# First mixer's recurrence in another order: row exponents one step ahead, norm factors right behind their moments, two half output tiles between the chunks

## The reference

```python
def even_mixer(h, w_in, w_out, sinks, conv_w, conv_b, i_bias, f_bias, ml_norm):
    p = h @ w_in
    ...
    y_att = sliding_window_sink_attention(q, k, v, sinks)
    ...
    hm = mlstm_chunkwise(q_m, k_m, v_m, log_i, log_f)
    hm = head_layernorm(hm, ML_NORM_EPS).reshape(bsz, T, ML_V_W) * ml_norm.astype(F32)
    y_ml = (hm * jax.nn.sigmoid(o_m.astype(F32))).astype(h.dtype)
    return jnp.concatenate([y_att, y_ml], axis=-1) @ w_out

# mlstm_chunkwise, 4 chunks of 128 tokens, 4 heads:
    C_loc = jnp.einsum('bnlh,bnlhk,bnlhv->bnhkv', wgt, kc, vc)
    C_new = fa[..., None, None] * C + fb[..., None, None] * Cl      # scan over the chunks
    w_intra = jnp.exp(dlog - m_t[:, :, :, None, :])
    w_inter = jnp.exp(inter_log - m_t)
    qk = jnp.einsum('bnthd,bnshd->bntsh', qc, kc) * w_intra
    num = jnp.einsum('bntsh,bnshv->bnthv', qk, vc) + w_inter[..., None] * jnp.einsum('bnthk,bnhkv->bnthv', qc, C_prev)
    h = num / jnp.maximum(jnp.abs(den), jnp.exp(-m_t))[..., None]
```

## Time and profile before

| | us |
|---|---|
| median of 3 runs | 1400.3 |
| lowest, highest | 1399.03, 1401.03 |
| the profiled execution | 1397.91 |
| its span in the profile | 1395.7 |
| PE busy in the span | 1324.3 (95%) |
| POOL, DVE, ACT busy | 662.4, 572.2, 537.6 |

### The profile page before, as it was taken

One profiled execution on the slowest core, in us unless ns is written; L12 is line 12 of the kernel. 1 busy time (PEld: TensorE's weight loads), 2 busy tenths in 40 slices (PEclk: granted clock), 3 DMA queues, 4 the chain that ended last, 5 costly groups with the idle time before them and its releaser, 6 DMA issues.

```text
span 1395.7 us, 17823 instructions
## 1 busy us (share of the span) xinstructions
PE 1324.3 (95%) x6461; PEld 1060.2 (76%) x6461; DVE 572.2 (41%) x917; ACT 537.6 (39%) x880; POOL 662.4 (47%) x813
## 2 busy tenths in 40 slices
PE   5999878999999999999798999888999999999997
PEld 4777656788888888887476778888878888888886
DVE  4537655421221211345679956365542121121233
ACT  5335654332322323335653436433443132231332
POOL 4653224554555545664343532321455555555552
PEclk9999978999999999999899999999999999999999
DMA  9322101333333333332212211000233333333331
GB/s 277 91 76 61 61 1 46 92 91 98 98 91 91 90 99 97 90 90 79 73 46 61 76 56 37 1 2 1 61 95 102 91 91 91 93 102 90 91 91 61
DMA packets 198034, 109.12 MB, mean 78 GB/s; under 512 B 4570, under 2 KB 195280, under 8 KB 197840
## 3 DMA queue, kind: packets, MB, share of 16 engines
q1 hardware_dynamic: 197552, 108.16, 26.4%
q0 software_dynamic: 416, 0.07, 0.0%
HBM read 106.11 MB, written 2.10 MB: 78 GB/s over the span
## 4 chain that ended last, share of the span: by engine, by line
PE 84%; DVE 9%; ACT 4%; issue 2%; DMA 0%; POOL 0%; DVEq 0%; SPq 0%; ACTq 0%
PE ps L878 23%; PE ps L879 23%; PE ps L880 23%; PE ps L865 2%; PE ps L919 1%; PE ps L920 1%; PE ps L921 1%; DVE arena L2273 1%; DVE late L2486 1%; PE ps L1283 1%; PE ps L1297 1%; PE ps L1036 1%; PE ps L1308 1%; PE ps L1165 1%; DVE arena L2559 0%
## 5 line engine op out<-in xcount | busy, mean ns | idle before, releaser
L782 POOL TENSOR_TENSOR w_lo<-raw_w,w_hi 128x256 fp32r<-128x256 f32 x760 | 616.4, 842 | 610.9 <-ACT w_hi L1405 610.9
L1405 ACT ACTIVATE w_hi<-raw_w 128x1024 fp32r<-128x1024 f32 x190 | 201.1, 1059 | 548.8 <-PE ps L880 439.7
L878 PE MATMUL ps<-hn_hi,w_hi 128*128 128x512 f32 x880 | 358.2, 407 | 3.0 <-POOL w_lo L782 2.1
L879 PE MATMUL ps<-hn_lo,w_hi 128*128 128x512 f32 x880 | 350.3, 398 | 0.0
L880 PE MATMUL ps<-hn_hi,w_lo 128*128 128x512 f32 x880 | 350.1, 398 | 0.0
L878 PE MATMUL ps<-hid_hi,w_hi 128*128 128x512 f32 x576 | 228.4, 397 | 0.0
L880 PE MATMUL ps<-hid_hi,w_lo 128*128 128x512 f32 x576 | 228.4, 396 | 0.0
L879 PE MATMUL ps<-hid_lo,w_hi 128*128 128x512 f32 x576 | 228.4, 396 | 0.0
L878 PEld LDWEIGHTS ps<-hn_hi,w_hi 128*128 128x128 f32 x880 | 167.1, 190 | 52.1 <-issue 10.6
L879 PEld LDWEIGHTS ps<-hn_lo,w_hi 128*128 128x128 f32 x880 | 166.9, 190 | 41.7 <-issue 2.9
L880 PEld LDWEIGHTS ps<-hn_hi,w_lo 128*128 128x128 f32 x880 | 166.7, 189 | 40.7
(11 more groups left out here) (376 smaller groups left out, 1343.5 us busy)
## 6 DMA issues: line engine op xcount, KB each, us to landing
raw_w<-in_w_up SPq DMA_DIRECT2D x64, 512.0 KB, 3.9
raw_w<-in_w_down SPq DMA_DIRECT2D x64, 512.0 KB, 3.6
raw_w<-in_o_w_in SPq DMA_DIRECT2D x27, 512.0 KB, 3.6
raw_w<-in_e_w_in SPq DMA_DIRECT2D x19, 512.0 KB, 3.6
raw_w<-in_e_w_out SPq DMA_DIRECT2D x8, 512.0 KB, 3.6
raw_w<-in_o_w_out SPq DMA_DIRECT2D x8, 512.0 KB, 3.4
rwkv_raw<-in_x SPq DMA_DIRECT2D x4, 512.0 KB, 8.1
out<-arena SPq DMA_DIRECT2D x8, 256.0 KB, 2.9
```

The source lines that it names most:

```text
L782: nc.gpsimd.tensor_tensor(w_lo[:, n % CUT, ks], raw_w[:, n % RING, ks], w_hi[:, n % CUT, ks].bitcast(F32), ALU.subtract).then_inc(w_cut, 1)
L878: mm(o, a_hi, b_hi, start=(k == 0), stop=False)
L879: mm(o, a_hi, b_lo, start=False, stop=False)
L1405: A(w_hi[:, n % CUT], raw_w[:, n % RING], ACT.Copy).then_inc(w_high, 1)
```

## The change

No instruction is added or removed on any engine; four things move.

1. ScalarE's list in `even_front`: `q_exp 1` goes from unit 7 to the end of unit 6, `w_exp 0` from unit 8 to unit 7. `w_exp 1` stays in unit 8. `w_exp` 2 and 3 leave units 9 and 10 and go behind the four copies of `hid_hi`, which become an item of their own (`att_high`).
2. TensorE's list and the plan of banks come from a new generator, `even_chunks`: `half_tile` 0 stands between `c_loc 2` and `num 2`, `half_tile` 1 between `qk_st 3` and `num 3`, 2 and 3 at the end.
3. VectorE: weights 1 and moments 0 come before the `low_first` four. `ml_gains(0)` stands between the second and third of these. Every later gains n follows its own moments n at once.
4. GpSimd: instead of four times L799 and then three times L806, each gain multiply is followed by the multiply with its normed chunk.

```diff
@@ -202,14 +202,28 @@
         if u == 9:
             for a in range(2):
                 yield "k_tok", a
-        if u == 7:
+        if u == 6:
             yield "q_exp", 1
-        if u == 8:
-            yield "w_exp", 0
-            yield "w_exp", 1
+        if u in (7, 8):
+            yield "w_exp", u - 7
         if u in (9, 10):
             yield "q_exp", u - 7
-            yield "w_exp", u - 7
+    yield "att_high", 0
+    yield "w_exp", 2
+    yield "w_exp", 3
+
+
+def even_chunks():
+
+    for n in range(NT):
+        yield "qk_st", n
+        if n < NT - 1:
+            yield "c_loc", n
+        if n >= 2:
+            yield "half", n - 2
+        yield "num", n
+    yield "half", 2
+    yield "half", 3
 
 
 def odd_front():
@@ -331,17 +345,18 @@
...
-            for n in range(NT):
-                for par in range(2):
-                    put("qk_st", n, par, bank=5 + par)
-                if n < NT - 1:
-                    put("c_loc", n, bank=7)
-                for par in range(2):
-                    put("num", n, par, bank=1 + 2 * (n % 2) + par)
-                if n == 1:
-                    put_out(0, 0)
-            for j in range(1, 4):
-                put_out(0, j)
+            for item in even_chunks():
+                kind, n = item
+                if kind == "half":
+                    put_out(0, n)
+                else:
+                    for par in range(2):
+                        if kind == "qk_st":
+                            put(kind, n, par, bank=5 + par)
+                        elif kind == "num":
+                            put(kind, n, par, bank=1 + 2 * (n % 2) + par)
+                    if kind == "c_loc":
+                        put(kind, n, bank=7)
             put_turned(0, "y_ml")
@@ -798,14 +813,14 @@
                         for t in range(NT):
                             nc.gpsimd.tensor_tensor(o_gate[:, t, :], o_gate[:, t, :], row("ml_norm", 512), ALU.mult
                                                     ).then_inc(S["o_gained"], 1)
-                        for t in range(NT - 1):
-
-                            pool.wait_ge(S["o_gained"], t + 1)
-                            drained(pool, "num", t, 0)
-                            drained(pool, "num", t, 1)
-                            nc.gpsimd.tensor_tensor(o_gate[:, t, :], o_gate[:, t, :],
-                                                    w_ml[:, t].rearrange("p h t -> p (h t)"), ALU.mult
-                                                    ).then_inc(S["y_ml_gated"], 1)
+                            if t < NT - 1:
+
+                                pool.wait_ge(S["o_gained"], t + 1)
+                                drained(pool, "num", t, 0)
+                                drained(pool, "num", t, 1)
+                                nc.gpsimd.tensor_tensor(o_gate[:, t, :], o_gate[:, t, :],
+                                                        w_ml[:, t].rearrange("p h t -> p (h t)"), ALU.mult
+                                                        ).then_inc(S["y_ml_gated"], 1)
                     if n == base["out", 1] + CUT - 1:
 
                         def zero_inverses(n):
@@ -1069,17 +1084,20 @@
                 for j in range(4):
                     drained(pe, "v", j)
                 pe.wait_ge(S["v_ones"], 1)
-                for n in range(NT):
+                for kind, n in even_chunks():
                     tok = slice(n * P, (n + 1) * P)
...
-                    if n < NT - 1:
+                    if kind == "half":
+                        half_tile(0, n, 0)
+                    elif kind == "qk_st":
+                        o = [free(pe, "qk_st", n, par) for par in range(2)]
+                        for a in range(2):
+                            for par in range(2):
...
+                    elif kind == "c_loc":
                         pe.wait_ge(S["k_scaled"], 1)
...
-                    pe.wait_ge(S["qkw_ready"], n + 1)
-                    o = [free(pe, "num", n, par) for par in range(2)]
...
-                    if n == 1:
-                        half_tile(0, 0, 0)
-                for j in range(1, 4):
-                    half_tile(0, j, 0)
+                    else:
+                        pe.wait_ge(S["qkw_ready"], n + 1)
...
@@ -1615,15 +1630,16 @@
                     ins.then_inc(free_sem("m_row", u), 1)
                     drained(act, "m_row", u)
                     act.sem_inc(S["wi_made"], 1)
+                elif kind == "att_high":
+                    for i in range(8):
+                        drained(act, "att", i)
+                    for k in range(4):
+                        A(hid_hi[:, k, :], y_mix[:, k, :], ACT.Copy).then_inc(high, 1)
                 elif kind == "w_exp":
                     act.wait_ge(S["wl_ready"], u + 1)
                     for j in range(4):
                         ins = A(w_ml[:, u, j, :], mtmp[:, u % 2, j * P:(j + 1) * P], ACT.Exp, bias=gg[:, u, j:j + 1])
                     ins.then_inc(S["n_keep"], 1)
-            for u in range(8):
-                drained(act, "att", u)
-            for k in range(4):
-                A(hid_hi[:, k, :], y_mix[:, k, :], ACT.Copy).then_inc(high, 1)
             for j in range(4):
                 drained(act, "o", j)
             A(o_gate, o_gate, ACT.Sigmoid).then_inc(S["o_sig"], 1)
@@ -2219,15 +2235,17 @@
                                        ).then_inc(S["ml_normed"], 1)
 
             ml_weights(0)
+            ml_weights(1)
+            ml_moments(0)
             for k in range(4):
                 low_first(0, k, y_mix[:, k, :])
-            for n in range(NT):
+                if k == 1:
+                    ml_gains(0)
+            for n in range(1, NT):
                 if n + 1 < NT:
                     ml_weights(n + 1)
-                if n:
-                    ml_gains(n - 1)
                 ml_moments(n)
-            ml_gains(NT - 1)
+                ml_gains(n)
             drained(dve, "num", NT - 1, 0)
             drained(dve, "num", NT - 1, 1)
             dve.wait_ge(S["o_gained"], NT)
```

48 lines of the change are left out of this document (23 added, 25 removed).

## The result

| | before | after |
|---|---|---|
| median, us | 1400.3 | 1392.28 |
| lowest, highest of 5 runs | 1398.29, 1401.42 | 1391.94, 1393.55 |
| the profiled execution | 1397.91 | 1392.26 |
| its span | 1395.7 | 1390.0 |

The ratio is 0.9947, with a 95% interval of 0.9936 to 0.9958: 8.0 us faster at the median, where 10.0 was forecast and 4.3 to 14 was the range. By the ratio the gain is 7.4 us, between 5.9 and 9.0. The two profiled executions lie only 5.65 us apart. Both numbers have to be explained, and the second gap is part of the lesson.

A forecast was written before the change was run, and what follows sets the result against it. TensorE, 95% busy, was taken as the bound, with waits and half clock from 170 to 225 us. Front, VectorE/ScalarE chain, port waits and TensorE backlog put T at 215.3, 10.0 us earlier: 1390.3 us, range 1386.3 to 1396.0.

The forecast's parts named there:

- case (D): Whole kernel: the author's own forecast, a gain between 6.5 and 12 us; chance 0.61.
- the chain: Recurrence, VectorE and ScalarE: weights, moments, roots and gains chunk by chunk up to the last gated chunk, done at 214.0 us.
- T: Start of TensorE's turn of the gated chunks after the recurrence; claimed to move from 225.34 to 215.3, 10.0 us.
- Front: Before the recurrence: row exponents of chunk 1 in unit 6 free bank 4 sooner; `qk_st 0` 3.4 us earlier.
- First root: ScalarE in the recurrence: first possible root at 193.75 us, which VectorE's gains 0 wait for.
- num 2: TensorE in the recurrence: starts at 197.9 us instead of 205.22, behind `half_tile` 0 at half clock.
- Port waits: Recurrence: VectorE's tiny rows wait while GpSimd multiplies; 0.8 us for each of three chunks, 2.4 us, ends 0 and 4.
- TensorE's backlog: Recurrence: late `num 3` at half clock adds some 1.3 us; the last half tiles end at 214.9, right before T.
- Behind T: Everything after T shifts alike; a clock drop from TensorE waiting there left at 0 to 3 us, for the range.
- The cover of the weight cut: After T: ScalarE cuts the next weight slot later, but 1.9 us of cover before TensorE needs it hides that.
- Rival A: Front and recurrence: clock stays high, TensorE is never late, T at 212.3, gain 13, median 1387.3; chance 0.22.
- Rival C: Recurrence: a late first root holds TensorE inside `half_tile` 0; slower, 1402.5 us with the root at 206; chance 0.03.

The follow-up runs named there:

- busy_twice: Changed kernel with extra unread matmuls filling TensorE's waits, 16 before the turn of the gated chunks and 12 before unit 6's turn; median 1391.27 us, ratio 0.9944.
- recurrence_alone: Changed kernel with the exponents of chunk 1 and weight exponents 0 and 1 back in units 7 and 8; median 1396.5 us, ratio 0.9960.
- low_four: Changed kernel with all four low parts ahead of gains 0 on VectorE; median 1390.77 us, ratio 0.9931.
- changed_again: The changed kernel itself, unedited, run again with a second profile; median 1391.62 us.
- gains_first: Changed kernel with GpSimd's old order, four gain multiplies and then three with the normed chunks; median 1390.21 us, ratio 0.9933.

## Why the prediction was right, and where its steps were not

The result lies in the range and the forecast's case (D) held; 10.0 was 2.0 us too much. The sum has three slips of its own. The terms of the chain, 211.4 + 1.50 + 0.78, give 213.7 and not 214.0. `num 3` at 208.5 is 1.4 us behind 207.1, where the text says 1.1 and then 1.3. And the three worst terms of the high end leave a gain of 5.0 and not 4.3. The first two nearly cancel (T at 215.1), and the third only widens the range. Step by step:

- **Front** (3.4 us, between 3.0 and 5.1): the mechanism is right, the size was too large. The loss to half clock is there (1.7 counted, 1.6 measured), and `qk_st 0` at 181.57 was luck, an execution that doesn't pay it (`busy_twice`, with the wait filled, 181.73). Eight other profiles with the same front have 183.1 to 184.1, where I put 183.0. Counted from the start of unit 7's scores on TensorE (166.95 before, 166.67 after), `qk_st 0` comes after 18.8 to 19.4 us with the old front (three profiles), after 16.35 to 16.54 with the new one and half clock, and after 14.9 without the fall: a gain of 2.2 to 3.1 us with the fall. What was put at nothing are the 0.6 us by which VectorE's norm of unit 6 now comes later, beside GpSimd's multiply of q; so the wait left is 2.96 us and not 2.5. The medians give the front alone 4.0, with 1.8 to 4.5 by the interval.
- **First root** at 193.75: 192.79. From `qk_st 0` that is 11.22 against 10.75, half a us longer. That ScalarE counts now, and VectorE waits at gains 0 (2.10 us), was right.
- **`num 2`** at 197.9: 196.23, which is 14.66 us behind `qk_st 0` where the sum had 14.9, mostly at half clock as taken (granted clock 0.51 from 195.5 to 199).
- **Port waits** (0.8 us three times, 2.4): under-sized. Measured 0.84 (L2190) + 1.04 + 0.83 + 1.03 = 3.7 us. I had the last pair block one row; it blocked two, one for each multiply. The bound of 4 held. Before, the same kind of wait summed to 4.3 us, 2.7 of it in moments 0.
- **TensorE's backlog** (1.3 us): failed. I had `num 3` at half clock and the last half tiles up to 214.9, right before T. They ran at full clock and ended at 210.5. What I had called work beside the chain was an idle stretch of 3.71 us.
- **T**: 32.3 us behind `qk_st 0` by the sum (215.3 less 183.0), 32.68 measured. The port waits' 1.3 us too little and the backlog's 1.3 us too much cancelled each other, which is luck; what is left is the root (0.5) less the slip in the sum (0.3), and 0.2 us stay unexplained.
- **Behind T** (0 in the sum, 0 to 3 for the range): this is the term of the sum that was mis-sized. It measured 3.06 us in after, 3.17 in `recurrence_alone` and 2.2 in `low_four`, each behind a wait of 3.71 us, and 0 in `changed_again` (wait of 2.16 us), `gains_first` (0.99) and the runs that keep TensorE busy. It follows from the failed step above it. With `num 3` and the half tiles at full clock my own numbers give 205.3 + 1.7 + 5.9 = 212.9 for the end of the half tiles against 214.0 for the chain (an estimate with the lengths of after's rows), so an idle TensorE was to be seen, of a third of the real length. I had named the fall as possible and kept it out of the sum. The cover of the weight cut held.
- **Rival A** (gain 13, clock high) has the clock that after's first profile shows up to T, except around `num 2`, but no price for the idle TensorE that follows from it. **Rival C** did not occur: the root was on time.

On the whole: 4.8 us of front and 6.3 of recurrence brought T forward by 11.1, then 3.1 went to the clock behind T, 2.4 to the variation of the rest, and 5.65 are left between the two profiles. At the medians 8.0 are left. Where the clock falls only profiled executions show. That it differs between executions of one kernel shows in the mean granted clock of every run: in `recurrence_alone` 0.980 goes with 1390.6 and 1391.1 us, 0.977 to 0.978 with 1394.0 to 1397.2. How often it falls at which place was not measured.

## What to carry to other kernels

When a chain of small steps is shortened so that TensorE finishes its side work first, its idle time moves to the place just before the hand-over, and in some executions the work behind it is then done at half clock: compare, for both orders, when the side work ends with when the chain ends, and price the difference at the lower clock. Put small VectorE work into a wait that is foreseen (here 1.8 us at T for one line, not separated at the medians). When a step moves, look at what its followers on other engines will then run beside (here 0.6 us). Let GpSimd's long multiplies start beside VectorE's rows that read PSUM, not beside its tiny rows with two inputs in SBUF. When two profiles disagree with the medians, compare distances between landmarks, and don't give the change credit or blame for stretches that it doesn't touch.

## What the runs showed of the hardware that I had not expected

- Where the clock falls is not fixed by the kernel. Behind the same wait of 2.96 us the front took 8.18 us in one execution and 9.76 in another of the same kernel. T to h took 9.53 and 6.49, behind waits of 3.71 and 2.16 us. A fall costs 1.6 us at the front and 3.1 behind T, or nothing where TensorE has slack.
- A pair of GpSimd multiplies back to back blocks two neighbouring rows of four elements per partition one after the other, 0.99 and 1.20 us instead of 0.16 and 0.17. GpSimd's own row is stretched too at times: 1.45 us beside VectorE's L2190 and 1.81 beside its low parts, where it takes 1.27.
- The part of the program that no kernel here changes took between 1163.9 and 1170.3 us, and all of the difference lies in the second mixer.
